# Expert outputs weighted when they are copied out and added into the residual by accumulating gathers, with a hinted branch behind the expert loop

## The reference, cut to what matters

```
logits = (x @ w_router).astype(jnp.float32)
top_v, top_i = lax.top_k(logits, TOP_K)
top_w = jax.nn.softmax(top_v, axis=-1)
gates = jnp.sum(jax.nn.one_hot(top_i, N_EXPERTS, dtype=jnp.float32) * top_w[..., None], axis=-2)
out = jnp.zeros_like(x)
for e in range(N_EXPERTS):
    out = out + gates[..., e:e + 1].astype(x.dtype) * swiglu(x, w_gate[e], w_up[e], w_down[e])
...
x = layer_norm(alpha * x + f, ln_ffn_g[i], ln_ffn_b[i])
x = x + (p[i] @ w_ple_proj[i]) * jax.nn.sigmoid(x @ w_ple_gate[i])
```

## Time and profile before

| | us |
|---|---|
| median of 3 runs (2201.53 to 2204.88) | 2201.73 |
| the profiled execution | 2201.86 |
| its span, first to last instruction | 2200.1 |
| what lies around the span | 1.76 |
| PE busy | 2166.8 (98%) |
| DVE busy | 1727.7 (79%) |
| ACT busy | 1415.6 (64%) |
| POOL busy | 61.3 (3%) |
| expert loop on PE | 464.75 to 1416.75 |

### The profile page before, as it was taken

One profiled execution on the slowest core, in us unless ns is written; L12 is line 12 of the kernel. 1 busy time (PEld: TensorE's weight loads), 2 busy tenths in 40 slices (PEclk: granted clock), 3 DMA queues, 4 the chain that ended last, 5 costly groups with the idle time before them and its releaser, 6 DMA issues.

```text
span 2200.1 us, 30875 instructions
## 1 busy us (share of the span) xinstructions
PE 2166.8 (98%) x11392; PEld 1810.2 (82%) x11392; DVE 1727.7 (79%) x1980; ACT 1415.6 (64%) x1582; POOL 61.3 (3%) x96
## 2 busy tenths in 40 slices
PE   9999999999999999999999999999999999999998
PEld 6788897778888888888888887779978898988888
DVE  6766656688888888888888889768668886776887
ACT  6644444667777777777777777656566556565554
POOL 3000000020000000000000002000000000000000
PEclk9999999999999999999999999999999999999999
DMA  9855555369999999999999999853144554224451
GB/s 382 291 187 185 183 192 184 113 268 391 368 390 368 394 373 386 375 386 374 382 381 376 384 371 392 319 190 116 69 151 183 192 191 157 77 107 156 189 189 60
DMA packets 83523, 573.26 MB, mean 261 GB/s; under 512 B 9744, under 2 KB 10368, under 8 KB 18224
## 3 DMA queue, kind: packets, MB, share of 16 engines
q1 hardware_dynamic: 77760, 545.29, 64.8%
q0 software_dynamic: 5376, 26.12, 3.3%
q10 hardware_dynamic: 288, 0.52, 0.1%
HBM read 564.03 MB, written 17.83 MB: 264 GB/s over the span
## 4 chain that ended last, share of the span: by engine, by line
PE 91%; DVE 4%; ACT 2%; issue 1%; DMA 1%; SPq 0%; POOL 0%; DVEq 0%; ACTq 0%; POOLq 0%
PE bank L831 67%; PE bank L899 10%; PE bank L901 5%; DVE w_lo L542 1%; PE bank L1190 1%; PE bank L1315 1%; PE bank L1325 1%; ACT arena L1532 1%; PE bank L1230 1%; PE bank L800 1%; DMA raw<-in_wu_qkv 1%; ACT w_hi L537 1%; PE bank L954 0%; DVE arena L2090 0%; PE bank L946 0%
## 5 line engine op out<-in xcount | busy, mean ns | idle before, releaser
L542 DVE TENSOR_TENSOR w_lo<-raw,w_hi 128x2048 fp32r<-128x2048 f32 x505 | 1156.2, 2300 | 248.0 <-ACT w_hi L537 246.2
L537 ACT CAST w_hi<-raw 128x2048 fp32r<-128x2048 f32 x505 | 964.5, 1912 | 357.8 <-PE bank L831 275.5
L831 PE MATMUL bank<-w_hi,xT 128*128 128x512 f32 x2368 | 750.8, 392 | 5.6 <-DVE w_lo L542 3.5
L831 PEld LDWEIGHTS bank<-w_hi,xT 128*128 128x128 f32 x2368 | 444.6, 188 | 106.5 <-issue 6.1
L831 PE MATMUL bank<-w_lo,xT 128*128 128x512 f32 x1184 | 461.0, 389 | 0.0
L831 PE MATMUL bank<-w_hi,aT_hi 128*128 128x512 f32 x864 | 344.4, 399 | 1.0 <-DVE w_lo L542 1.0
L899 PE MATMUL bank<-xT,w_hi 128*128 128x512 f32 x960 | 339.6, 398 | 0.9 <-issue 0.4
L831 PE MATMUL bank<-w_hi,aT_lo 128*128 128x512 f32 x864 | 337.4, 390 | 0.0
L831 PE MATMUL bank<-w_lo,aT_hi 128*128 128x512 f32 x864 | 336.6, 390 | 0.0
L901 PE MATMUL bank<-xT,w_lo 128*128 128x256 f32 x960 | 269.3, 280 | 0.0
L831 PEld LDWEIGHTS bank<-w_lo,xT 128*128 128x128 f32 x1184 | 222.5, 188 | 44.8 <-issue 0.5
(11 more groups left out here) (349 smaller groups left out, 1698.6 us busy)
## 6 DMA issues: line engine op xcount, KB each, us to landing
raw<-in_wu_eg SPq DMA_DIRECT2D x112, 1024.0 KB, 7.1
raw<-in_wu_eu SPq DMA_DIRECT2D x112, 1024.0 KB, 7.2
raw<-in_wu_ed SPq DMA_DIRECT2D x112, 1024.0 KB, 7.1
raw<-in_wu_up SPq DMA_DIRECT2D x44, 1024.0 KB, 4.8
raw<-in_wu_ffn_gu SPq DMA_DIRECT2D x28, 1024.0 KB, 4.8
raw<-in_wu_in SPq DMA_DIRECT2D x28, 1024.0 KB, 4.9
raw<-in_wu_down SPq DMA_DIRECT2D x22, 1024.0 KB, 4.8
raw<-in_wu_ffn_d SPq DMA_DIRECT2D x14, 1024.0 KB, 4.8
```

The source lines that it names most:

```text
L537: nc.scalar.copy(w_hi[:, place(i), :], src).then_inc(*E.hi.mark("unit", i))
L542: nc.vector.tensor_tensor(w_lo[:, place(i), :], raw[:, i % RAW, :], w_hi[:, place(i), :].bitcast(F32), ALU.subtract) \
L831: mm = nc.tensor.matmul(o, l[i], r[j], start=(first and n == 0), stop=(last and n == 2), skip_group_check=not lone)
```

## The change

- **Weights at copy-out.** The two weights of each token are scattered by POOL into a small HBM tensor `wg`, by slot and expert, and one DMA loads them as `w_slot`, 128 slots by 2 tiles by 8 experts. In each turn DVE copies one column of it into `w_now`, and ACT's copy-out of banks 0 and 1 becomes a scaled activation.
- **Accumulating gathers.** POOL's scaling and adding go. In the last turn POOL issues four gathers that add to `R` as they land: the tokens' first rows for both tiles, then, each when the first has landed, the second rows. A row of the eighth expert isn't there yet; its index is replaced by row 0, which holds zeros.
- **The last expert by a product.** A 0/1 matrix from token to slot (`last`) is made by DVE ahead of the loop, transposed by PE and copied by ACT (`back`). Behind the loop PE multiplies it with `ye` into banks 0 to 3 (`last_rows`, four float32 products of 512 columns), and `take_rows` adds the bank to `R`. The store of the last rows, the two gathers behind it and SP's waits for them go.
- **The hinted branch.** The branch over the overflow code is written as compare and branch with a prefetch hint, issued at the top of each turn of PE's loop. ACT, DVE, SP and POOL keep theirs unhinted.
- **PE's order.** Of the eight embedding products, two move behind the transposes of tile 0, in place of the two idle products of 256 columns.
- **Zeros.** DVE's `memset` of `ye` ahead of the loop goes to POOL, ahead of its scatters.

```diff
+            def weights():
+                gp.wait_ge(*y_rows_ready.at())
+                for k, w in enumerate((w1, w2)):
+                    for t in range(NT):
+                        gp.indirect_dma_start(wg, bass.IndirectOffsetOnAxis(ap=w_rows[:, 2 * t + k:2 * t + k + 1], axis=0),
+                                              w[:, t:t + 1], None).then_inc(*wg_put.mark("all"))
+                gp.wait_ge(*wg_put.at("all"))
+                gp.dma_start(moe["w_slot"], wg.rearrange("(h r e) o -> r h (e o)", r=P, e=NE)).then_inc(*w_in.mark())
             def collect():
-                gp.wait_ge(*y_rows_ready.at())
                 gp.wait_ge(*M.put.at("before"))
...
-                for t in range(NT):
-                    fetch(0, t, low_in)
-                gp.wait_ge(*low_in.last())
                 gp.wait_ge(*M.act.at("scaled"))
-                for t in range(NT):
-                    y = moe["y"][:, 0, t, :]
-                    nc.gpsimd.tensor_scalar(y, y, wlo[:, t:t + 1], None, ALU.mult).then_inc(*low_scaled.mark(t))
-                for t in range(NT):
-                    gp.wait_ge(*low_scaled.at(t))
-                    nc.gpsimd.tensor_tensor(R[:, t, :], R[:, t, :], moe["y"][:, 0, t, :], ALU.add).then_inc(*low_added.mark(t))
-                gp.wait_ge(*M.put.at("last"))
-                for t in range(NT):
-                    fetch(1, t, high_in[t])
+                for k in range(2):
+                    for t in range(NT):
+                        if k:
+                            gp.wait_ge(*rows_in[t].at(0))
+                        gp.indirect_dma_start(R[:, t, :], None, yg,
+                                              bass.IndirectOffsetOnAxis(ap=y_rows[:, 2 * t + k:2 * t + k + 1], axis=0),
+                                              compute_op=ALU.add).then_inc(*rows_in[t].mark(k))
...
+            gp.wait_ge(*x_ready.at(1, "mix", 1))
+            nc.gpsimd.memset(moe["ye"], 0.0).then_inc(*zeroed.mark())
             dispatch()
+            weights()
...
+            def last_rows():
+                pe.wait_ge(*M.free[1].at("last", "members"))
+                for t in range(NT):
+                    for nb in range(2):
+                        pe.wait_ge(*M.free[nb].at("moe", "ye", nb))
+                        o = open_bank(M, 2 * t + nb)
+                        nc.tensor.matmul(o[:, :], moe["back"][:, t, :], moe["ye"][:, nb * 512:(nb + 1) * 512], start=True, stop=True) \
+                            .then_inc(*M.groups.mark("last", "rows", t, nb))
...
                     with pe.Fori(0, NE) as e:
+                        overflow_skip = pe.mark_branch_hint_location()
...
-                    with pe.If(r > 0):
+                    pe.br_lt(r, 1, on_true="pe_past_overflow", on_false="pe_overflow").branch_hint(overflow_skip)
+                    with nc.body("pe_overflow", valid_engines=[mybir.EngineType.PE]):
...
+                ac.wait_ge(*E.dve.at(tag, "weight"))
                 for h in range(2):
-                    nc.scalar.copy(moe["ye"][:, h * 512:(h + 1) * 512], bank[h][:, :]).then_inc(*E.free[h].mark(tag, "ye", h))
+                    nc.scalar.activation(results[E][:, h * 512:(h + 1) * 512], bank[h][:, :], ACT.Identity, scale=w_now[:, 0:1]) \
+                        .then_inc(*E.free[h].mark(tag, "ye", h))
...
+                    if f == 1:
+                        ve.wait_ge(*w_in.at())
+                        ve.wait_ge(*turn_before(E.free[1], tag, "ye", 1))
+                        step(V_.tensor_copy(w_now, moe["w_slot"][:, tile:tile + 1, e]), E, tag, "weight")
...
                     def take_rows(t, nb, total):
-                        ve.wait_ge(*high_in[t].at(t))
-                        ve.wait_ge(*low_added.at(t))
+                        ve.wait_ge(*rows_in[t].at(1))
+                        ve.wait_ge(*M.groups.at("last", "rows", t, nb))
                         cols = slice(nb * 512, (nb + 1) * 512)
-                        chain(V_.scalar_tensor_tensor(R[:, t, cols], moe["y"][:, 1, t, cols], whi[:, t:t + 1], R[:, t, cols],
-                                                      ALU.mult, ALU.add, accum_out=total))
+                        V_.scalar_tensor_tensor(R[:, t, cols], bank[2 * t + nb][:, :], 1.0, R[:, t, cols],
+                                                ALU.mult, ALU.add, accum_out=total).then_inc(*M.free[2 * t + nb].mark("last", "rows", t, nb))
```

102 lines of the change are left out of this document (60 added, 42 removed).

## The result

The changed kernel takes 2228.8 us (median of four runs, 2227.92 to 2230.77), the kernel before 2201.78; the ratio is 1.0117, with a 95% interval of 1.0105 to 1.0129. Forecast were 2196.7 us.

What follows compares the result with a forecast made beforehand. PE, busy in nearly all of the span, was taken as the bound. Terms -2.40, -2.75 and +0.13 sum to -5.02 us from the profiled 2201.86; the median lies 0.13 lower, so 2196.7 us, range 2195.8 to 2201.5.

Steps and rivals of the forecast that it cites:

- Rival C: Expert loop: the hint's block pushes out a loop block, PE gaps about 4 us every turn; 31.8 us, 2228.5 us; chance 0.06.
- POOL's work out of the eighth turn, -2.40 us: Eighth turn: without POOL's scaling and adding slowing DVE's splits, it takes the seventh's 118.60 us instead of 121.00.
- rival B: Eighth turn: the gathers starve the weight stream, units land too late; 2198.3 to 2204.7 us; chance 0.18.
- the double weight: Eighth turn: if an adding gather weighs double, weight units land after 19.9 us, over by 8.
- They go in pairs: Eighth turn: argument against starved weights, gathers run in pairs one after the other, two left 1.6 us; cost taken as 0.
- The last rows by a product, -2.75 us: Behind the loop: DVE's first `take_rows` starts 2.5 us earlier, and reading a bank saves 0.25 us more.
- The hint, 0 in the loop and PE in time behind it: PE's branch: one hidden sequencer instruction a turn, 0 us; behind the loop PE is ready 0.5 us before `x_half`.
- Rival A: Branch behind the loop: the hint does nothing, PE's branch still takes 3.98 us and transposes come later; 2200.8 us; chance 0.15.
- ACT's scaled copy-out stays a pass over the same elements: 0: Each loop turn: scaling in ACT's copy-out adds no time, 0 us.
- `w_slot` in time: First turn: weights scattered and loaded are ready at 497.6 us, before DVE's wait at 498.6; cost 0.
- Loop entry and `memset`: Ahead of the loop: two new PE transposes lose 0.13 us; the `memset` moved to POOL costs 0.
- The range's lower end: Whole kernel: 2195.8 us, with DVE's fetch of code being shorter taken as -0.5 us.

Runs made afterwards that it cites:

- after_iota: The changed kernel without its new table entry, numbers 0 to 7 read from the existing `iota`, so tiles are back in place: 2206.1 us against 2203.35, ratio 1.0014.

## Why the prediction was wrong, step by step

- **The step that failed is one that isn't in it.** The prediction costs PE, DVE, ACT, POOL and the queues, and says nothing of the new table entry; by silence it took an allocation to be free. It costs 25.4 us in the kernel before (2203.81 to 2229.18, in one round) and 22.7 in the changed kernel (2206.1 to 2228.8), five times all the gains that were forecast: each product that streams weights takes 233 ns from start to start and not 227.
- **Rival C gave 2228.5 us and the measured time is 2228.8. That is chance.** Its mechanism, a code block missed each turn, would show as 4 us of idle PE in every turn. PE is idle in none of the turns two to seven, its queue moved five instruction blocks in the first turn, as before, and none in the seven others, and without the hint nothing came back. A right number bears out no theory; the sign that the prediction had named for C was missing.
- **POOL's work out of the eighth turn, -2.40 us: right by itself, but given back.** DVE's splits take 2.28 to 2.30 us all through the changed kernel's loop, and with plain gathers the eighth turn is as short as the seventh. With adding ones it is 3.7 us longer than the seventh in after_iota (2.2 in the changed kernel). That is rival B, to which I gave 0.18. Its mechanism with the double weight is right, its price for that was too dear: landings of 16.5 us and not 19.9, 3.7 us lost and not 8. "They go in pairs" was no protection.
- **The last rows by a product, -2.75 us: right in kind, too large.** The transposes start 12.5 us behind the start of the last expert product in after_iota, 14.6 before: 2.1 us gained of the 2.6 forecast for that point. 0.5 are missing. (In the changed kernel itself it is 14.1, only 0.5 gained.) ACT's scaled passes put its last split, and with it DVE's, 0.3 us later; DVE's sequencer gets to its branch only behind the start of that split; and the gap behind it, which I took for the fetch of code, was then 3.1 us, and 4.8 in the changed kernel, instead of 2.9.
- **The hint, 0 in the loop and PE in time behind it: right.** PE's branch took 0.37 us, the clock stayed up, the transposes waited for `x_half` and not for PE. Rival A's other half was right too: without the hint it is 3.4 us more with the tiles in place (2.7 and 5.0 in the two other pairs), forecast 4.1.
- **"ACT's scaled copy-out stays a pass over the same elements: 0": wrong, 0.18 us a turn.** Same elements, but 686 ns instead of 592, with PE's next weights behind it. 1.5 us in all.
- **`w_slot` in time: right, at a price not counted.** The scatters' landing was costed as a date for DVE's wait, never as a load on the weight stream. The first turn lost between nothing and 3.8 us.
- **Loop entry and `memset`: small, the 0.13 us not to be told.** The `memset` took POOL 0.97 us at 450.6, and the loop was entered between 0.9 us sooner and 1.5 us later than before in after_iota and its seven variants with the same tiles.
- **The range's lower end has a slip.** 2196.7 less the 0.5 us for DVE's fetch is 2196.2, not 2195.8. It changes nothing in the outcome.

## What to carry to other kernels

Look at what an edit allocates before counting what it executes: one more entry in a table moves every tile behind it, and a shift that isn't a multiple of 256 bytes, against the tiles that the same products read, can outweigh the edit. The sign for it is an engine that is busy throughout and yet slower, with the same count of instructions at a few ns more each; the test is the old kernel with an unused pad. And a DMA that is "off the path" has a weight for the stream beside it, which its bytes don't tell. An adding gather shows it in its share of the DMA engines' time; scatters of single elements don't (0.3% above), so look at the traffic of all queues and at when the units beside them land.

## What the runs showed of the hardware that I had not expected

- A product's time depends on the distance between the tiles of x and of the weights in SBUF: from start to start 227 ns at a multiple of 256 bytes and 232 to 234 at 32, 64 and 128 bytes more, with 512 streamed columns of weights; 235 to 236 and 228 to 233 with 2 x 256 of x. What is best for the one kind is the worst for the other, and each can have its own.
- An adding gather takes the DMA engines twice as long a byte as a plain one (20.9 against 10.3% of 24 us for a MB), and brings their traffic from some 425 down to some 310 GB/s.
- Four scatters of 128 elements of 4 bytes can hold the whole DMA traffic at 19 to 58 GB/s for about 6 us.
- A branch hint given a whole turn of 118 us ahead took PE's branch from 5.2 to 5.8 us (4.0 in the kernel before) down to 0.37; the same on DVE did nothing.
- ACT's pass over 128 x 512 from a bank takes 686 ns with a scale taken from a column, 592 as a copy.
